# Expert weights laid eight rows to a partition in a two-layer diffusion step, with the down product from stationary weights

## The chip, the core and the metric

One core of a Trainium2 chip runs the whole step: TensorE (PE) with its weight loads (PEld), VectorE (DVE), ScalarE (ACT), GpSimd (POOL), SyncE (SP), and 16 DMA engines. The number of interest is the device time of one execution in microseconds; before the change the median of 3 runs is 2039.6 us. Everything is float32; PE runs each float32 product as two matmul instructions, each with its own weight load.

## The reference, cut to what matters

Two token sets, 128 context tokens and 512 latent tokens of width 1024, go through two layers. A layer is a combined input projection, a convolution module beside differential attention, an output projection, and a mixture of 16 experts in which each expert chooses 16 context rows and 64 latent rows. The convolution module and the experts are what the change touches:

```python
def conv_module(a, g, conv_w, conv_b, ln_g, ln_b):
    u = a * jax.nn.sigmoid(g)
    u = depthwise_conv(u, conv_w, width=31) + conv_b
    mu = jnp.mean(u, axis=-1); var = jnp.mean((u - mu) ** 2, axis=-1)      # over 512 channels
    return jax.nn.silu((u - mu) * lax.rsqrt(var + EPS) * ln_g + ln_b)

def expert_choice(h, w_router, w_gate, w_up, w_down):                      # per token set
    aff = jax.nn.softmax(h @ w_router)
    gsel, idx = lax.top_k(aff.T, C)                                        # C = 2*T/16 rows per expert
    xs = h[idx]                                                            # 80 rows over both sets
    hid = jax.nn.silu(xs @ w_gate[e]) * (xs @ w_up[e])                     # 1024 -> 1024
    ye = hid @ w_down[e] * gsel
    return zeros.at[idx].add(ye)                                           # every expert adds its rows
```

Each expert has three 1024x1024 matrices, 12.6 MB; both layers have 16 experts, 403 MB in all.

## The kernel before, in words

Tokens lie as 5 tiles of 128. The weights pass through `weight_ring`, six slots of 2 MB. SyncE issues all weight transfers, in the order of the code, each behind a wait that says that its slot is free.

**Projection.** `proj_unit` loads the input projection in five units of 512 columns. PE goes through 16 blocks (unit i, 128 columns b), in the order i then b: units 0 and 1 are the two halves of the gated convolution, units 2 and 3 keys and queries. For each block it does 512 latent and 128 context columns, and ACT copies the result out. From the ninth block on each block is followed by one unit of the modulation vectors (`block_modulation`). Five V blocks, one per token tile, follow (L500 before). DVE multiplies the gated halves (`glu_ready`), does the 31 taps over four chunks of 128 channels in place in `acc` (L1042), in between it rotates keys and queries (`rotate`). Behind the last V block come, one after the other: transposes of the context keys (L508), their copy by ACT (L815) into `key_rows`, which lies in `conv_tmp`, the store of it, and then, because the squares use `conv_tmp`, a wait for that store; PE's sums over channels for the mean (L519) and the squares (L527) with a matrix of ones; ACT's root, DVE's reciprocal (L1085) and product, ACT's SiLU (L834). Then attention begins, whose first exponential on ACT is the first L844.

**Experts.** An expert's weights are six units: gate and up for the first four row blocks, gate and up for the last four, and the two halves of down. `expert_src` lays row `k*128 + p` of a matrix on partition p, so a unit is 4 pieces of 4 KB on each partition. Unit i of the next expert is issued when unit i of this one is used (`expert_used`). The picked rows of the residual are gathered by POOL (80 rows of 4 KB), transposed on PE (L692), modulated by DVE. In gate and up (L706) the weights are stationary, 64 columns at a time on the two column halves of the array, and the 80 tokens move. In down (L722) the hidden rows are stationary (80 columns) and 512 weight columns move, so the result comes out with tokens on the partitions; DVE scales it (L1278) and POOL adds it to the residual in memory with an indirect DMA, then gathers for the expert after the next. PE's loop is `gate_up`, `picked_transposes(e + 1)`, `down`.

What sets the order is only the order of the code on each engine and the semaphores; there is no planner.

## Time and profile before

| what | value |
|---|---|
| median of 3 runs | 2039.6 us (2035.76 to 2039.83) |
| profiled execution, own time | 2046.08 us |
| its span, first to last instruction | 2044.3 us |
| PE busy / weight loads busy | 90% / 59% |
| DVE, ACT, POOL busy | 31%, 15%, 6% |
| bytes moved, mean rate | 534.68 MB, 262 GB/s |
| mean granted clock of PE | 0.951 |

The profile is of one execution. A busy PE is not a PE at its peak, since matmuls are pipelined and their ends are modelled. The page divides the span into 40 slices of 51 us; a digit is a busy share in tenths. The two long stretches of nines in the line of the DMA engines are the expert loops of the two layers.

### The profile page before, as it was taken

The numbers are of one execution on the slowest core, as the hardware profiler recorded it, in microseconds if no ns is written. First come the engines' busy times: TensorE is split into PE (matmuls) and PEld (weight loads), VectorE is DVE, ScalarE is ACT, GpSimd is POOL, SyncE is SP. The second block draws the span as 40 slices with busy tenths as digits, with TensorE's granted clock in tenths as the row PEclk, the third lists the DMA queues.
The fourth block names the chain that finished last, engine by engine and source line by source line (L and its number), as shares of the span: only waits on it lengthen the run. The fifth ranks groups of instructions, "written<-read, shape, count | busy, mean of one in ns | idle before, by whom it ended". The sixth has DMA issues, their size and how long they took to land.

```text
span 2044.3 us, 45797 instructions
## 1 busy us (share of the span) xinstructions
PE 1830.5 (90%) x21123; PEld 1202.4 (59%) x21123; DVE 632.7 (31%) x1044; ACT 306.6 (15%) x616; POOL 129.3 (6%) x157
## 2 busy tenths in 40 slices
PE   4999968894999999999949997789589999999993
PEld 2555436454676767767625553564376768677671
DVE  1159848234101101010120995752611011110101
ACT  2201145221000000000021112532200000000001
POOL 2000000000000000000010000000000000000001
PEclk9999989896999999999979999889799999999997
DMA  9336530233999999999931554004379999999995
GB/s 344 120 106 224 206 154 1 81 156 127 378 388 400 388 396 394 389 400 389 395 141 41 179 192 154 0 1 175 128 281 395 390 399 389 400 389 394 395 389 194
DMA packets 154438, 534.68 MB, mean 262 GB/s; under 512 B 5937, under 2 KB 6354, under 8 KB 154386
## 3 DMA queue, kind: packets, MB, share of 16 engines
q1 hardware_dynamic: 138880, 482.37, 61.3%
q0 software_dynamic: 12320, 42.47, 7.1%
q10 hardware_dynamic: 3186, 9.12, 1.1%
q8 instruction: 36, 0.59, 0.1%
q14 instruction: 16, 0.13, 0.0%
HBM read 509.30 MB, written 24.64 MB: 261 GB/s over the span
## 4 chain that ended last, share of the span: by engine, by line
PE 79%; DMA 8%; DVE 8%; ACT 1%; SPq 1%; issue 1%; POOL 0%; ACTq 0%; DVEq 0%; POOLq 0%
PE ps L706 25%; PE ps L722 19%; PE ps L488 14%; PE ps L618 7%; DMA weight_ring<-in_w_up_dram 5%; PE ps L500 3%; PE ps L432 2%; DVE neg_m L1112 2%; SPq L342 1%; PE ps L575 1%; PE ps L692 1%; PE ps L441 1%; PE ps L638 1%; DMA weight_ring<-in_conv_w_dram 1%; DMA out_dram<-conv_tmp 1%
## 5 line engine op out<-in xcount | busy, mean ns | idle before, releaser
L706 PEld LDWEIGHTS ps<-v_sb,weight_ring 128*64 128x64 f32 x16384 | 572.6, 138 | 37.5 <-issue 30.2
L706 PE MATMUL ps<-v_sb,weight_ring 128*64 128x80 f32 x16384 | 579.2, 234 | 11.6 <-DMA weight_ring<-in_w_up_dram 6.2
L722 PE MATMUL ps<-weight_ring,mix 128*80 128x512 f32 x1024 | 446.7, 594 | 0.0
L722 PEld LDWEIGHTS ps<-weight_ring,mix 128*80 128x80 f32 x1024 | 151.0, 150 | 272.5 <-issue 268.0
L488 PE MATMUL ps<-mix,weight_ring 128*128 128x128 f32 (+1 forms) x1024 | 284.5, 439 | 5.2 <-DVE mix L1012 5.2
L488 PEld LDWEIGHTS ps<-mix,weight_ring 128*128 128x128 f32 x1024 | 156.8, 192 | 142.0 <-issue 136.4
L1271 DVE TENSOR_TENSOR mix<-mix,ps 128x320 f32<-128x320 f32 x64 | 28.3, 483 | 544.3 <-PE ps L706 544.3
L1042 DVE SCALAR_TENSOR_TENSOR weight_ring<-u_gate,conv_cols,weight_ring 128x655 f32<-128x655 f32 x240 | 195.2, 898 | 0.0
L922 ACT ACTIVATE mix<-ps 128x320 f32<-128x320 f32 x64 | 24.5, 435 | 983.2 <-PE ps L706 983.2
L1278 DVE SCALAR_TENSOR_TENSOR qk<-ps,gsel,gate 80x1024 f32<-80x1024 f32 x32 | 41.0, 1280 | 392.3 <-PE ps L722 392.3
L618 PE MATMUL ps<-weight_ring,mix 128*128 128x512 f32 x320 | 144.6, 608 | 2.0 <-issue 2.0
L1401 POOL DMA_INDIRECT x_res<-qk,row_idx x32 | 45.9, 1434 | 979.9 <-DVE qk L1278 979.9
L618 PEld LDWEIGHTS ps<-weight_ring,mix 128*128 128x128 f32 x320 | 61.2, 195 | 74.3 <-issue 74.3
L500 PE MATMUL ps<-weight_ring,mix 128*128 128x512 f32 x160 | 70.5, 596 | 0.0
L1112 DVE TENSOR_REDUCE neg_m<-ps 128x2 f32<-128x1280 f32 (+1 forms) x40 | 50.8, 1274 | 17.4 <-PE ps L550 17.1
L844 ACT ACTIVATE weight_ring<-ps,neg_m 128x640 f32<-128x640 f32 (+1 forms) x80 | 55.7, 705 | 2.4 <-DVE neg_m L1112 2.3
L500 PEld LDWEIGHTS ps<-weight_ring,mix 128*128 128x128 f32 x160 | 29.8, 190 | 39.9 <-issue 39.9
L561 PE MATMUL ps<-ident,weight_ring 128*128 128x128 f32 x168 | 33.3, 305 | 22.0 <-DVE o_tok L1131 10.0
L432 PE MATMUL ps<-weight_ring,cond_silu 128*32 128x512 f32 x384 | 49.6, 637 | 0.8 <-issue 0.8
L1024 DVE TENSOR_TENSOR u_gate<-u_gate,conv_tmp 128x128 f32<-128x128 f32 (+1 forms) x16 | 7.2, 489 | 138.9 <-ACT conv_tmp L795 138.9
L575 PE MATMUL ps<-v_sb,weight_ring 128*128 128x128 f32 x272 | 45.4, 311 | 4.9 <-ACT weight_ring L862 4.8
L1171 DVE TENSOR_TENSOR conv_tmp<-ps,u_gate 128x1024 f32<-128x1024 f32 x10 | 12.2, 1224 | 103.7 <-PE ps L618 103.7
(176 smaller groups left out, 1185.8 us busy)
## 6 DMA issues: line engine op xcount, KB each, us to landing
weight_ring<-in_w_gate_dram SPq DMA_DIRECT2D x64, 2048.0 KB, 19.0
weight_ring<-in_w_up_dram SPq DMA_DIRECT2D x64, 2048.0 KB, 19.7
weight_ring<-in_w_down_dram SPq DMA_DIRECT2D x64, 2048.0 KB, 19.9
weight_ring<-in_w_mod_dram SPq DMA_DIRECT2D x24, 2048.0 KB, 8.2
weight_ring<-in_w_in_dram SPq DMA_DIRECT2D x10, 2048.0 KB, 12.8
weight_ring<-in_w_out_dram SPq DMA_DIRECT2D x4, 2048.0 KB, 10.6
x_res<-x_tile POOLq DMA_DIRECT2D x10, 512.0 KB, 3.3
x_unit<-x_norm ACTq DMA_DIRECT2D x10, 512.0 KB, 2.7
```

Source lines behind the costliest of these rows:

```text
L432: last = nc.tensor.matmul(ps[c * STRIP:(c + 1) * STRIP, 6, :], cond_silu[:, k, :], w[:, k, :], start=(k < 4), stop=(k >= 4))
L488: last = nc.tensor.matmul(ps[:, 2 * (n % 3) + bank, 0:cols.stop - cols.start], w[:, k, tokens(b)], mix[:, k, cols], start=(k == 0), stop=( ...
L500: last = nc.tensor.matmul(ps[:, 2 * (n % 3), :], mix[:, k, tokens(t)], w[:, k, :], start=(k == 0), stop=(k == KD - 1))
L575: last = nc.tensor.matmul(ps[:, 7, tokens(1)], a_col[:, tokens(j)], vals, start=(j == 0), stop=(j == n - 1))
L618: last = nc.tensor.matmul(ps[:, 2 * (i % 2) + n, :], mix[:, k, tokens(t)], w[:, k % 4, n * BANK:(n + 1) * BANK], start=(k == 0), stop=(k = ...
L706: last = nc.tensor.matmul(ps[c * HALF:(c + 1) * HALF, 2 * (i % 2) + f // BLK, f % BLK * CAP:(f % BLK + 1) * CAP], w[:, kk, o:o + HALF], pi ...
L722: last = nc.tensor.matmul(ps[0:CAP, 4 + n, :], hid[:, k, :], w[:, kk, n * BANK:(n + 1) * BANK], start=(k == 0), stop=(k == KD - 1))
L844: last = nc.scalar.activation(prob[:, b, m, 0:n], score_rows(s)[:, m, :], ACT.Exp, bias=neg_m[:, b, m:m + 1], accum_out=row_sum[:, b, m:m ...
L1042: ins = nc.vector.scalar_tensor_tensor(acc[:, j, :], src, w, acc[:, j, :], ALU.mult, ALU.add)
L1112: nc.vector.tensor_reduce(neg_m[:, s % 2, :], score_rows(s), AX, ALU.max, negate=True)\
L1278: nc.vector.scalar_tensor_tensor(added, ps[0:CAP, 4:6, :].rearrange("p b n -> p (b n)"), gsel[:, bass.ds(e, 1)], gate2[:], ALU.mult, ALU.m ...
L1401: nc.gpsimd.indirect_dma_start(out=x_res, out_offset=bass.IndirectOffsetOnAxis(ap=row_idx[:, e:e + 1], axis=0), in_=added, in_offset=None, ...
```

## The change

Six edits that belong together:

- A matrix of an expert is now laid with rows `8p` to `8p + 7` on partition p. Four of them are 16 KB in one piece, so a unit is one piece per partition. The contraction over rows then takes, for block k, the features `8q + k`; hidden features and picked rows follow: gate and up read their 64 stationary columns with a step of eight, and the picked rows, the normalized rows and the router's weights are read in the same order. The modulation vectors for it are brought into that order (`ROW_UNITS`, `par2_cols`).
- Down is computed as gate and up are: the weights stationary, 64 columns at a time, the 80 tokens moving. The result has features on the partitions; ACT copies its halves into `result_t`, PE transposes them back into the banks of the picked rows, and DVE takes them from there.
- PE's loop waits for the result of the expert before ahead of `picked_transposes`, because of those banks.
- The blocks of the projection go in the order of `BLOCK_LIST`: the gated pairs of the first two chunks come first. DVE does the taps of chunks 0 and 1, then those of 2 and 3.
- The sums for the mean stand behind V block 1, those of the squares behind V block 3; ACT and DVE follow. The cached keys are transposed before the V blocks.
- `key_rows` lies in the second half of `x_tile`, and POOL's load of that half waits for the store.

```diff
+BLOCK_LIST = ((0, 0), (1, 0), (0, 1), (1, 1), (0, 2), (0, 3), (1, 2), (1, 3)) + tuple(
+    (i, b) for i in (2, 3) for b in range(BLK))
-        key_rows = conv_tmp[:, 0, 0:BANK]
+        key_rows = x_tile[:, 1, 0:BANK]
             def expert_src(l, e, i):
                 w, half = (w_gate, w_up)[i % 2] if i < 4 else w_down, i // 2 if i < 4 else i - 4
-                return w[l, e].rearrange("(k p) n -> p k n", p=P)[:, half * 4:half * 4 + 4, :]
+                return w[l, e].rearrange("(p k) n -> p (k n)", p=P)[:, half * UNIT:(half + 1) * UNIT]
...
                 for i in range(2, 4):
-                    sp.wait_ge(*proj_done.at(l, BLK * (i - 1)))
+                    sp.wait_ge(*proj_done.at(l, block_no(i - 2, BLK - 1) + 1))
                     proj_unit(l, i)
...
-                for i in range(4):
-                    pe.wait_ge(*proj_loaded[i % 2].at(l, i // 2 + 1))
+                for n, (i, b) in enumerate(BLOCK_LIST):
+                    if b == 0:
+                        pe.wait_ge(*proj_loaded[i % 2].at(l, i // 2 + 1))
...
+                def conv_means():
+                    pe.wait_ge(*conv_ready.at(l, CH))
+                    if l == 0:
+                        pe.wait_ge(*past_copied.at(0, 1))
+                    for c0, c1, bank in ((LAT0, C_LEN, 1), (0, N_CTX, 3)):
+                        for j in range(CH):
+                            last = nc.tensor.matmul(ps[:, bank, 0:c1 - c0], ones[:], acc[:, j, c0:c1],
+                                                    start=(j == 0), stop=(j == CH - 1))
+                    last.then_inc(mean_ready.sem, 1)
+                def conv_squares():
+                    for j in range(CH):
+                        pe.wait_ge(*squared.at(l, j + 1))
+                        if j == 0:
+                            pe.wait_ge(*centred.at(l, CH))
+                        for c0, c1, bank in ((LAT0, C_LEN, 5), (0, N_CTX, 3)):
+                            last = nc.tensor.matmul(ps[:, bank, 0:c1 - c0], ones[:], conv_tmp[:, j % 2, c0:c1],
+                                                    start=(j == 0), stop=(j == CH - 1))
+                        last.then_inc(square_used.sem, 1)
...
                     block_modulation(l, n)
+                    if t == 1:
+                        conv_means()
+                    if t == 3:
+                        conv_squares()
...
-                                                   picked[:, tokens(k)], ident[0:CAP, 0:CAP])
+                                                   picked.rearrange("t (q k) -> t k q", k=KD)[:, k, :],
+                                                   ident[0:CAP, 0:CAP])
...
+                        cols = w.rearrange("p k (q f) -> p k f q", f=KD)
-                                        w[:, kk, o:o + HALF], picked_t[:, k, :],
+                                        cols[:, kk, f, c * HALF:(c + 1) * HALF], picked_t[:, k, :],
...
                 def down(e):
-                        for kk in range(KD // 2):
-                            k = half * (KD // 2) + kk
-                            for n in range(2):
-                                last = nc.tensor.matmul(ps[0:CAP, 4 + n, :], hid[:, k, :],
-                                                        w[:, kk, n * BANK:(n + 1) * BANK],
-                                                        start=(k == 0), stop=(k == KD - 1))
+                        for d in range(KD):
+                            for kk in range(KD // 2):
+                                k = half * (KD // 2) + kk
+                                for c in range(2):
+                                    o = d * P + c * HALF
+                                    last = nc.tensor.matmul(
+                                        ps[c * HALF:(c + 1) * HALF, 4 + d // BLK, d % BLK * CAP:(d % BLK + 1) * CAP],
+                                        w[:, kk, o:o + HALF], hid[:, k, :], ...)
+                            if half == 1 and d == BLK - 1:
+                                last.then_inc(result_lo_done.sem, 1)
                         last.then_inc(expert_used.sem, 1)
+                def result_transposes(e):
+                    pe.wait_ge(*picked_scaled.at(l, e + 2))
+                    for k in range(KD):
+                        if k % BLK == 0:
+                            pe.wait_ge(*result_copied.at(l, 2 * e + k // BLK + 1))
+                        last = nc.tensor.transpose(ps[0:CAP, 6 + k // BLK, tokens(k % BLK)], result_t[:, k, :], ident[:])
+                    last.then_inc(result_back.sem, 1)
                 with nc.Fori(0, EXPERTS, engines=[mybir.EngineType.PE], hint_back_edge=True) as e:
                     gate_up(e)
+                    pe.wait_ge(*result_taken.at(l, e + 1))
                     picked_transposes(e + 1)
                     down(e)
+                    result_transposes(e)
...
+                    for half in range(2):                                       # ACT, behind the SiLU
+                        ...
+                        nc.scalar.activation(result_t[:, half * BLK:(half + 1) * BLK, :], halves(4 + half), ACT.Copy)\
+                          .then_inc(result_copied.sem, 1)
...
-                act.wait_ge(*cache_stored.at(l, 2))
...
-                taps(0, TAPS // 2)
+                glu(0)
+                glu(1)
+                taps((0, 1), 0, TAPS)
+                glu(2)
+                glu(3)
+                taps((2, 3), 0, TAPS // 2)
                 rotate(0)
-                taps(TAPS // 2, TAPS)
+                taps((2, 3), TAPS // 2, TAPS)
...
-                    dve.wait_ge(*expert_used.at(l, e * 6 + 6))
+                    dve.wait_ge(*result_back.at(l, e + 1))
                     dve.wait_ge(*residual_written[0].at(l, e + 3))
-                    nc.vector.scalar_tensor_tensor(added, ps[0:CAP, 4:6, :].rearrange("p b n -> p (b n)"),
+                    nc.vector.scalar_tensor_tensor(added, ps[0:CAP, 6:8, :].rearrange("p b n -> p (b n)"),
...
-                for i in range(2):
-                    load_x(x_tile[:, i, :], l, OUT_TILES[i], x_loaded[i])
+                load_x(x_tile[:, 0, :], l, OUT_TILES[0], x_loaded[0])
+                pool.wait_ge(*cache_stored.at(l, 2))
+                load_x(x_tile[:, 1, :], l, OUT_TILES[1], x_loaded[1])
```

How rows move, at three places. A row is line, operation, result and operands, shape, count; the float32 doubling is not counted. First PE in layer 0 from the last V blocks on, before; L500 is a V block, L508 the key transposes, L417 the cached keys, L519 the mean, L527 the squares, L541 the first scores:

```order
L500 MATMUL ps<-weight_ring,mix 128x512 x8
L441 MATMUL ps<-pair_sum,x_tile 128x2 x4
L508 MATMUL ps<-ident,qk 128x128 x4
L417 MATMUL ps<-ident,x_norm 128x128 x8
L519 MATMUL ps<-weight_ring,ones 128x512 x4
L519 MATMUL ps<-weight_ring,ones 128x143 x4
L527 MATMUL ps<-conv_tmp,ones 128x512
L527 MATMUL ps<-conv_tmp,ones 128x143
L541 MATMUL ps<-qk 128x128 x6
```

and now, from V block 1 on (L547 a V block, L523 the mean, L534 the squares, L559 the key transposes, L575 the first scores):

```order
L547 MATMUL ps<-weight_ring,mix 128x512 x8
L464 MATMUL ps<-pair_sum,x_tile 128x2 x4
L445 MATMUL ps<-weight_ring,cond_silu 32x512 x8
L523 MATMUL ps<-weight_ring,ones 128x512 x4
L523 MATMUL ps<-weight_ring,ones 128x128 x4
L534 MATMUL ps<-conv_tmp,ones 128x512
L534 MATMUL ps<-conv_tmp,ones 128x128
L559 MATMUL ps<-ident,qk 128x128 x4
L575 MATMUL ps<-qk 128x128 x6
```

Between L523 and L534 stand two more V blocks with their modulation, and one behind L534. The mean and the squares have moved from behind the V blocks to between them, each with 15 columns fewer.

PE in the expert loop, before, from gate and up to the loop's end:

```order
L706 MATMUL ps<-v_sb,weight_ring 64x80 x256
L690 ISA
L692 MATMUL ps<-ident,qk 128x80 x8
L717 ISA
L722 MATMUL ps<-weight_ring,mix 80x512 x8
L717 REGISTER_ALU
L722 MATMUL ps<-weight_ring,mix 80x512 x8
L728 REGISTER_ALU
```

and now (L742 gate and up, L727 the picked rows, L759 down, L772 the transposes of the result):

```order
L742 MATMUL ps<-v_sb,weight_ring 64x80 x256
L725 ISA
L727 MATMUL ps<-ident,qk 128x80 x8
L752 ISA
L759 MATMUL ps<-mix,weight_ring 64x80 x64
L752 REGISTER_ALU
L759 MATMUL ps<-mix,weight_ring 64x80 x64
L772 MATMUL ps<-ident,mix 80x128 x8
L776 REGISTER_ALU
```

Down has 128 small products where it had 16 large ones, with the weights in the stationary place, and eight transposes behind them.

DVE in layer 0, before, from the last gated product to the second rotation (L1024 gating, L1037 and L1042 taps, L1053 to L1058 a rotation):

```order
L1024 TENSOR_TENSOR u_gate<-u_gate,conv_tmp 128x512
L1037 TENSOR_SCALAR weight_ring<-u_gate,conv_cols,par_cols 128x655 x4
L1042 SCALAR_TENSOR_TENSOR weight_ring<-u_gate,conv_cols,weight_ring 128x655 x56
L1053 STREAM_SHUFFLE weight_ring<-qk 128x512 x4
L1055 TENSOR_TENSOR qk<-qk,cos_sb 128x4x512
L1042 SCALAR_TENSOR_TENSOR weight_ring<-u_gate,conv_cols,weight_ring 128x655 x64
```

and now (L1100 gating, L1112 and L1117 taps, L1128 on a rotation):

```order
L1100 TENSOR_TENSOR u_gate<-u_gate,conv_tmp 128x512
L1112 TENSOR_SCALAR weight_ring<-u_gate,conv_cols,par_cols 128x655 x2
L1117 SCALAR_TENSOR_TENSOR weight_ring<-u_gate,conv_cols,weight_ring 128x655 x60
L1100 TENSOR_TENSOR u_gate<-u_gate,conv_tmp 128x128
L1112 TENSOR_SCALAR weight_ring<-u_gate,conv_cols,par_cols 128x655 x2
L1117 SCALAR_TENSOR_TENSOR weight_ring<-u_gate,conv_cols,weight_ring 128x655 x28
L1128 STREAM_SHUFFLE weight_ring<-qk 128x512 x4
L1117 SCALAR_TENSOR_TENSOR weight_ring<-u_gate,conv_cols,weight_ring 128x655 x32
```

The taps of two chunks now stand before the gating of the other two.

## Rows read from the trace of the kernel before

**Rows 1.** The page: busy tenths and GB/s in 40 slices of the span.
```profile
PE   4999968894999999999949997789589999999993
...
...
DMA  9336530233999999999931554004379999999995
GB/s 344 120 106 224 206 154 1 81 156 127 378 388 400 388 396 394 389 400 389 395 141 41 179 192 154 0 1 175 128 281 395 390 399 389 400 389 394 395 389 194
```

**Rows 2.** Chain of waits, layer 0, first two experts: start us, us, what.
```profile
495.82 20.09 PE ps L706 x512
...
530.55 17.86 PE ps L706 x512
...
549.11 13.94 PE ps L722 x32
```

**Rows 3.** The same chain, the last two experts of layer 0.
```profile
908.70 27.19 DMA weight_ring<-in_w_up_dram
...
976.53 26.51 DMA weight_ring<-in_w_up_dram
...
1022.39 0.03 issue
```

**Rows 4.** Busy time by window; last columns granted clock, DMA share, GB/s.
```profile
495.82:502.70 6.88, 6.88 (x140) 6.88 (x142) 0.00 (x0) 0.00 (x0) 0.00 (x0) 0.69 0.17 49
...
530.00:540.00 10.00, 10.00 (x276) 9.52 (x276) 1.28 (x1) 0.00 (x0) 2.41 (x2) 1.00 0.95 307
...
905.00:927.00 22.00, 22.00 (x254) 12.59 (x252) 3.72 (x5) 0.00 (x0) 2.34 (x2) 1.00 1.03 410
928.00:936.00 8.00, 7.13 (x208) 6.97 (x204) 0.00 (x0) 0.87 (x3) 0.00 (x0) 1.00 1.04 344
...
1018.00:1024.00 6.00, 4.38 (x11) 1.27 (x9) 1.28 (x1) 0.00 (x0) 0.00 (x0) 1.00 1.05 387
```

**Rows 5.** SyncE's own queue in the timeline: start us, us, what.
```profile
502.69 0.39 SPq L342 DMA_DIRECT2D weight_ring<-in_w_gate_dram  x1
...
908.70 4.16 SPq L342 DMA_DIRECT2D weight_ring<-in_w_up_dram  x1
```

**Rows 6.** Groups by form (layer 0's loop), and a row of the chain.
```profile
L922 ACT ACTIVATE mix<-ps 128x320 f32<-128x320 f32 x32 | 12.2, 435 | 491.5 <-PE ps L706 491.5
...
456.33 1.69 PE ps L638 x16
```

**Rows 7.** Chain of waits, layer 1, from the last V block to attention.
```profile
1249.79 3.45 PE ps L500 x8
...
1253.76 0.61 ACT conv_tmp L815
...
1254.39 7.48 DMA out_dram<-conv_tmp
...
1270.92 4.26 DVE weight_ring L1085
...
1276.08 4.47 ACT mix L834 x8
...
1280.57 1.28 ACT L844
...
1281.86 0.81 ACT weight_ring L844 x4
```

**Rows 8.** Chain (layer 0) and timeline (DVE's taps, layer 1's mean).
```profile
55.34 79.81 PE ps L488 x288
...
227.14 7.06 PE ps L500 x16
...
274.74 6.42 PE ps L527 x16
...
185.25 52.03 DVE L1042 SCALAR_TENSOR_TENSOR weight_ring<-u_gate,conv_cols,weight_ring 128x655 f32<-128x655 f32 x64
...
1253.91 4.68 PE L519 MATMUL ps<-weight_ring,ones 128*128 128x512 f32 x16 [0.25 <-ACT v_sb L806]
```

190 lines of the change are left out of this document (114 added, 76 removed).

## The prediction, made before the changed kernel was run

> **What bounds the kernel now.** I read the page's slices first, then the chain of waits in order of time, then the windows with the DMA rate. In the slices [rows 1] two long stretches, one per layer, have PE and DMA both at 9 and the rate at 378 to 401 GB/s: the expert loops, some 1,054 of 2,044 us (526.6 in layer 0, 495.82 to 1022.39, [rows 2, 3], and as much in layer 1). Which of the two engines bounds them the slices cannot say. The chain gives PE: an expert takes 17.86 (gate and up) + 0.70 (transposes of the picked rows) + 13.94 (down) = 32.50 us, over and over [rows 2]. But late in the loop it leaves PE: it waits for the last up unit, which landed at 908.70 + 27.19 = 935.89 and at 976.53 + 26.51 = 1003.04, two experts apart, so the weights come at 33.58 us an expert [rows 3]. That is the true period. Weights alone move at 410 GB/s, 2 MB in 5.12 us, and while the scatter and gather of rows are in flight at 344 [rows 4]; 6 x 5.12 = 30.7, so the row transfers cost 2.9 us an expert. The DMA falls 1.08 us behind PE per expert, and the one expert of weights held in the ring hides that until the end. SyncE shows it too: an issue takes 0.39 us at 502.69 and 4.16 us at 908.70, as if its queue were full [rows 5]. So **the expert loops are DMA-bound**, and a faster PE alone gains there only at the two ends.
>
> Outside, the chain has a stretch in which PE is nearly idle: from the end of the last V block (1249.79 + 3.45 = 1253.24) to the first exponential (1281.86) 28.6 us pass in layer 1 [rows 7], and the same steps stand in layer 0: a copy of the keys, 7.48 us of waiting for its store, squares, root, reciprocal, normalization, SiLU, one after the other.
>
> **The change, part by part.** All sums are made on the profiled execution: span 2044.3, own time 2046.08, which is 6.5 over the median of 2039.6; I carry the difference over to the median.
>
> *Convolution norm inside the V blocks.* PE now does the sums for the mean (4.68 us, [rows 8]) after V block 1 and those of the squares (6.42, [rows 8]) after block 3. The last V block thus ends 4.7 + 6.4 = 11.1 us later, in layer 1 at 1264.3. The squares end one block earlier, at 1264.3 - 7.9 = 1256.4. Table load 1.28 and root 0.9 on ACT: 1258.6; reciprocal 4.26 on DVE: 1262.9; first normalized quarter 0.85 later, 1263.7, so it is ready before ACT is free of the last V copy, 1264.9. Then table load 1.28, SiLU 4.47, key copy 0.61 and table load 1.28: first exponential at 1272.5 instead of 1281.86, 9.3 us earlier. Layer 0 has the transposes of the cached keys and some constants in the same line, which moves a little of it; I take 8.5 there. The store of the keys is no longer waited for, since they lie in x_tile. Its cover: the load of the second x_tile half now waits for that store, about 100 us before its use. The sum needs DVE to be done with the taps by V block 1. They ended at 185.25 + 52.03 = 237.3, 64 of them at 0.81 us each [rows 8]. With the new block order two gated chunks are ready after four blocks instead of eight, at 55.34 + 4 x 8.87 + 1.2 = 92 (nine blocks took 79.81); 62 taps end near 142, the other half with the first rotation between near 205, the second rotation near 224, and PE gets to the mean at 227.14 + 7.06 + 3.7 = 238 [rows 8]. If that cover failed, each us would be paid in full on PE. Together **-17.8 us**.
>
> *Down from stationary weights.* It leaves 32 instructions of 436 ns (13.94 us) and adds 256 of the form of gate and up, 128x64 stationary and 80 columns moving; 512 of these take 17.86, so 8.93 us. Added behind it: ACT's copy of the last 320 columns (435 ns, [rows 6]), four transposes of about 0.11 us (16 matmul instructions with 128 stationary columns took 1.69 us, [rows 6]), two semaphore hops: 1.4 us. PE period 17.86 + 0.70 + 8.93 + 1.4 = 28.9. DVE's gated result waits for the transposes, and the scatter for it; both have some 20 us to spare inside the loop. What it gains is at the ends. At the start: from the first reload's issue at 502.69 [rows 5] to 1003.04 the DMA brought 14.67 experts' units, 34.1 us each instead of 33.58, so 7.8 us were lost in the first expert or two. Some of it is the first transfer's own delay; some is that units 4 and 5 came free late (530 to 540: share 0.95 and 307 GB/s, where rows and weights together give 344, [rows 4]). With down 5 us shorter I take 2.5 us a layer. At the end the last unit lands two units after 1003.04, at 1013.3, and PE ended at 1022.39; now 1013.3 + 4.5 + 1.4 = 1019.2: 3.2 a layer. **-11.4 us** for both layers.
>
> *16 KB pieces.* A unit was 512 pieces of 4 KB, now 128 of 16 KB. No row shows 16 KB, but rows of two sizes bound it [rows 4]: 2 KB pieces (the input projection) go at 387 GB/s (84.7 ns a piece on each of 16 engines), 4 KB at 410 (159.8 ns). The difference, 75.1 ns for 2 KB, leaves 10 ns fixed per piece. 16 KB: 10 + 8 x 75.1 = 611 ns, 429 GB/s, a unit in 4.89 us. If a 16 KB piece is handled as four of 4 KB nothing is gained (5.12); if long pieces read in steps of 32 KB suit the memory less, the nearest row is the 2 KB rate, 5.42. I take 4.92, a little short of this line through two points. 0.20 us x 90 units (15 reloads of 6) x 2 layers: **-36 us**. The period becomes 6 x 4.92 + 2.9 = 32.4, over PE's 28.9, so it stays DMA-bound with 3.5 us to spare.
>
> *Gate and up columns with a step of eight.* Each of 512 weight loads an expert now takes every eighth column, 32 bytes apart. No row of this trace has such a read. Today two halves of 64 columns and their matmuls pass in 2 x 34.9 = 69.8 ns. A load of 128 packed columns is seen at 1.69/16 = 106 ns, so 64 take 53 and are hidden under 67 ns of 80 moving columns. From below, the strided load costs nothing (nor can it gain, the matmul being the longer). From above, it takes twice the time: 106 ns for a pair of halves, if they still load side by side. It would begin to count at 83 ns a pair, where PE reaches 32.4. I take zero. The strided transposes of picked and normalized rows (8 an expert, 8 a token tile) go the same way at a tenth of the size.
> The Trainium skill speaks against this part: "Advanced Engine Details and Errata", section Memory Cachelines, says that SBUF has lines of 16 bytes, that at least two hits on one are needed to absorb the access latency, and that going to another line with each access costs. Four-byte elements 32 bytes apart hit each line once. By that rule the upper bound holds; what it makes of the time is the second rival below. No row here shows it either way.
>
> *Small edits* (layout of the second modulation and norm vectors, four more short loads at 35 us, the wait for the third projection unit two blocks later): the unit is issued two blocks, 17.7 us, before its use, more than three times the 5.4 us that its bytes take. Nothing.
>
> **Sum**: 17.8 + 11.4 + 36 = 65; 2046.1 - 65 = 1981 for a profiled execution, **1974** for the median.
>
> **Rivals.**
> *A. The pieces gain nothing* (chance 0.22). The queue cuts them to 4 KB, or the rate is capped elsewhere. For: the rows have two sizes only, and both lie between 387 and 410. Against: the fixed part between them. Time: 2039.6 - 29 = 2010.
> The Trainium skill, "DMA: Bandwidth & Descriptors", section SWDGE vs HWDGE vs iDMA, puts a packet at 4096 bytes by preference; by that rule this rival wins. The trace neither agrees nor disagrees: it has no piece above 4 KB.
> *B. The strided weight load is paid* (0.16), the slower side. For: nothing hides more than 17 ns of a pair's load. Against: nothing in the trace. Price: 256 pairs x (106 + 3) ns = 27.9 us instead of 17.86, PE period 38.9. A layer's loop runs 16 x 38.9 + 2.2 (the slow first expert, 20.09 against 17.86 [rows 2]) = 625 instead of 526.6 from first matmul to last. 2 x 98 - 18 = +178: 2218. It decides from 83 ns a pair on; just past it the change is worth about the first and last terms only.
> *C. The row transfers interleave better or the fixed part is larger* (0.07): a unit at 4.8, time near 1950.
> *D. Longer pieces are read more slowly* (0.05): at 5.42 a unit, 0.3 x 180 = 54 - 29 = +25: 2065.
> *E. PE's waits gather in one gap.* While rows are in flight a unit needs 7.8 us and PE 4.5, so it idles 3.3 us once an expert. The granted clock was 0.69 in the first 6.9 us of the loop, behind a stretch in which PE had waited, and 1.00 after it [rows 4]: 1.2 and 2.4 GHz in turn. If each expert pays the 2.2 us of the first, PE needs 31.1, under 32.4; only the ends lose 2 or 3 us. Inside the range.
>
> **Chances and range.** Forecast with its spread (unit 4.85 to 5.05) 0.50, A 0.22, C 0.07, B 0.16, D 0.05. About 0.2% (4 us) is what a measurement of this kernel can tell from no change. Slower: B and D, 0.20, with 0.02 given back because a load only partly slowed is hidden: 0.18. Same: 0.03. Faster: 0.79. The range 1950 to 2034 holds the forecast, A and most of C; B stays outside.
>
> **What would show it.** Right: DMA issues of 16 KB pieces landing 4.9 us apart late in a loop, near 425 GB/s; the chain in the loop going through weight transfers and SyncE, no longer through PE; PE rows of 128x64 with a mean as before and pairs 70 ns apart; PE idle some 3 us an expert, waiting for the last up unit; first exponential 8.5 to 9.3 us earlier after the projection's start. Wrong: packets of 4 KB in the size line (A); gate and up over 21 us an expert with the chain in PE throughout (B); V blocks waiting for DVE's taps.

## The result, and the profile after

| what | before | after |
|---|---|---|
| median | 2039.0 us (4 runs) | 2335.6 us (4 runs, 2334.5 to 2341.45) |
| ratio of the runs | | 1.146, 95% interval 1.144 to 1.149 |
| profiled execution, own time | 2046.08 us | 2334.59 us |
| its span | 2044.3 us | 2332.6 us |
| PE busy / weight loads busy | 90% / 59% | 92% / 77% |

The change made the kernel 14.6% slower; 1974 was forecast, with a range to 2034. Rival B named the mechanism and undersized it (2218). Where a kernel's executions fell into a faster and a slower group, as only those of experiment ten did, its time and ratio below are those of the faster group.

The page's slices, which answer to [rows 1]:

```profile
PE   4999888879999999999959997895999999999994
...
DMA  9156403348888888888622613043788888888872
GB/s 355 53 190 231 171 13 126 135 173 318 306 316 307 300 327 308 303 324 303 241 87 86 214 70 127 1 167 131 296 317 314 300 327 307 300 322 301 314 291 96
```

In the loops PE still stands at 9, but the DMA engines have fallen to 8 and to 300 to 327 GB/s. The loops are no longer bound by the weights. The chain of waits in layer 0's loop (start us, us, what; answers to [rows 2, 3]) says by what:

```profile
526.91 31.28 PE ps L742 x511
558.19 1.04 PE ps L727 x8
559.23 9.00 PE ps L759 x256
568.24 1.17 PE ps L772 x8
569.41 0.04 issue
569.45 31.27 PE ps L742 x511
```

It never leaves PE. Gate and up (L742) take 31.27 us where they took 17.86 [rows 2], that is 122.1 ns for each of 256 pairs of halves instead of 69.8. Down (L759) takes 9.00, against 13.94 before and 8.93 as worked out. An expert needs 42.54 us (526.91 to 569.45) where the weights had set 33.58.

The groups by form name the instruction (line, engine, operation, tiles, shape, count | busy us, mean ns | idle before):

```profile
L742 PEld LDWEIGHTS ps<-v_sb,weight_ring 128*64 128x64 f32 x16384 | 996.8, 218 | 13.3 <-issue 13.3
L742 PE MATMUL ps<-v_sb,weight_ring 128*64 128x80 f32 x16384 | 1001.5, 285 | 5.2 <-DVE v_sb L1350 3.9
L759 PEld LDWEIGHTS ps<-mix,weight_ring 128*64 128x64 f32 x8192 | 285.5, 137 | 3.3 <-issue 0.7
L759 PE MATMUL ps<-mix,weight_ring 128*64 128x80 f32 x8192 | 290.9, 233 | 0.5 <-issue 0.5
```

The same load, 128 rows by 64 columns of float32, has a mean of 137 ns from packed columns (down) and of 218 from every eighth column (gate and up). Loads and matmuls overlap, so a mean is not the time between two starts. But the load's busy time, 996.8 us, has become as long as the matmul's, which is what to expect if the load now paces the pair; experiment one tests it. The copy of the result on ACT costs 438 ns in the mean, where 435 was taken from its neighbour [rows 6].

A window in the loop (PE, PEld, DVE, ACT, POOL busy; then granted clock, DMA share, GB/s; answers to [rows 4]):

```profile
530.00:540.00 10.00, 10.00 (x170) 10.00 (x170) 0.00 (x0) 0.00 (x0) 1.61 (x2) 1.00 1.01 315
```

The clock is granted in full (1.00) there, as it was before; it is not the cause. PEld was busy 9.52 of 10 us in the window at 530 before, now 10.00. SyncE's queue and the issues answer to [rows 5]:

```profile
925.58 0.33 SPq L355 DMA_DIRECT2D weight_ring<-in_w_up_dram  x1
```

```profile
weight_ring<-in_w_gate_dram SPq DMA_DIRECT2D x64, 2048.0 KB, 7.5
```

Late in the loop an issue takes 0.33 us where it took 4.16, and over the whole run a gate unit lands 7.5 us after its issue (median) where it took 19.0: little is queued ahead of it.

The convolution's end in layer 1, in the chain, answers to [rows 7, 8]:

```profile
1397.28 4.49 PE ps L534 x16
1401.77 6.88 PE ps L547 x16
...
1408.67 0.60 ACT v_sb L874
...
1417.23 0.82 ACT weight_ring L905 x4
```

The wait for the store and the reciprocal have gone out of the chain. From the end of the last V block to the first exponential 8.6 us pass (1408.65 to 1417.23) where 28.6 did.

**The account.** The stretches between five marks (the projection's first matmul, first and last exponential, first matmul of the loop and last of down), in both profiled executions:

| stretch, us | before L0, L1 | after L0, L1 | difference |
|---|---|---|---|
| start to projection | 55.3 | 50.3 | -5.0 |
| projection to first exponential | 236.4, 224.9 | 229.9, 218.7 | -12.7 |
| exponentials, and on to the loop | 204.1, 206.5 | 203.6, 204.7 | -2.3 |
| expert loop | 526.6, 527.0 | 679.9, 680.7 | +307.0 |
| behind the loop | 33.3, 30.2 | 33.6, 31.3 | +1.4 |

The mark "first exponential" is here the start of its table load, 1.3 us ahead of the exponential itself. The sum is +288.4, the difference of the spans 288.3. The first row is no effect: over the kernels below this stretch lasts 50.2 to 56.7 us without a pattern. The second scatters as well, by some 1.7 us a layer between kernels that have the same code there. All that was lost was lost in the loop.

### The profile page after: what moved, and what is told of

Its sections match the earlier page's. It is cut to its first block, busy times and chain, and to the rows that moved or that the text cites. A ratio compares the mean times of both kernels' runs of the same rounds, so it can differ in the third digit from the quotient of the medians.

```text
span 2332.6 us, 60929 instructions
## 1 busy us (share of the span) xinstructions
PE 2141.9 (92%) x28611; PEld 1795.3 (77%) x28611; DVE 636.0 (27%) x1063; ACT 335.3 (14%) x690; POOL 131.3 (6%) x161
## 4 chain that ended last, share of the span: by engine, by line
PE 88%; DVE 7%; DMA 2%; ACT 1%; issue 1%; POOL 0%; ACTq 0%; DVEq 0%; POOLq 0%
PE ps L742 43%; PE ps L759 12%; PE ps L510 12%; PE ps L652 6%; PE ps L547 3%; PE ps L445 2%; PE ps L772 2%; PE ps L727 2%; DVE neg_m L1197 1%; PE ps L609 1%; PE ps L673 1%; DMA weight_ring<-in_conv_w_dram 1%; PE ps L458 1%; DVE weight_ring L1233 1%; PE ps L595 1%
## 5 line engine op out<-in xcount | busy, mean ns | idle before, releaser
L742 PEld LDWEIGHTS ps<-v_sb,weight_ring 128*64 128x64 f32 x16384 | 996.8, 218 | 13.3 <-issue 13.3
L742 PE MATMUL ps<-v_sb,weight_ring 128*64 128x80 f32 x16384 | 1001.5, 285 | 5.2 <-DVE v_sb L1350 3.9
L759 PE MATMUL ps<-mix,weight_ring 128*64 128x80 f32 x8192 | 290.9, 233 | 0.5 <-issue 0.5
L759 PEld LDWEIGHTS ps<-mix,weight_ring 128*64 128x64 f32 x8192 | 285.5, 137 | 3.3 <-issue 0.7
L1117 DVE SCALAR_TENSOR_TENSOR weight_ring<-u_gate,conv_cols,weight_ring 128x655 f32<-128x655 f32 x240 | 195.3, 894 | 0.0
L983 ACT ACTIVATE mix<-ps 128x320 f32<-128x320 f32 x64 | 24.5, 434 | 769.8 <-PE ps L742 769.8
L991 ACT ACTIVATE mix<-ps 128x320 f32<-128x320 f32 x64 | 28.0, 438 | 532.3 <-PE ps L759 532.3
L547 PE MATMUL ps<-weight_ring,mix 128*128 128x512 f32 x160 | 70.6, 595 | 0.0
L547 PEld LDWEIGHTS ps<-weight_ring,mix 128*128 128x128 f32 x160 | 29.7, 190 | 36.5 <-issue 36.5
L595 PE MATMUL ps<-ident,weight_ring 128*128 128x128 f32 x168 | 32.8, 300 | 22.3 <-DVE o_tok L1216 10.0
L727 PE MATMUL ps<-ident,qk 80*128 80x80 f32 x272 | 38.2, 286 | 9.7 <-DMA qk<-x_unit,row_idx 9.7
```

Source lines behind the costliest of these rows:

```text
L547: last = nc.tensor.matmul(ps[:, 2 * (n % 3), :], mix[:, k, tokens(t)], w[:, k, :], start=(k == 0), stop=(k == KD - 1))
L595: last = nc.tensor.transpose(dst, a_row[:, s % 2, tokens(j)], ident[:])
L727: last = nc.tensor.transpose(ps[:, 6 + k // 4, (k % 4) * CAP:(k % 4 + 1) * CAP], picked.rearrange("t (q k) -> t k q", k=KD)[:, k, :], iden ...
L742: last = nc.tensor.matmul(ps[c * HALF:(c + 1) * HALF, 2 * (i % 2) + f // BLK, f % BLK * CAP:(f % BLK + 1) * CAP], cols[:, kk, f, c * HALF: ...
L759: last = nc.tensor.matmul(ps[c * HALF:(c + 1) * HALF, 4 + d // BLK, d % BLK * CAP:(d % BLK + 1) * CAP], w[:, kk, o:o + HALF], hid[:, k, :] ...
L1117: ins = nc.vector.scalar_tensor_tensor(acc[:, j, :], src, w, acc[:, j, :], ALU.mult, ALU.add)
```

## The experiments

Medians stand against 2038 to 2040 us for the kernel before, measured beside them. Experiments two to six are one execution each. The cuts of code show the lines that matter; `...` stands for other lines, and where nothing else is said they are against the changed kernel.

### One: the columns packed, all else as changed

```diff
-                                        cols[:, kk, f, c * HALF:(c + 1) * HALF], picked_t[:, k, :],
+                                        w[:, kk, f * P + c * HALF:f * P + (c + 1) * HALF], picked_t[:, k, :],
```

> The changed kernel with one edit: gate and up read 64 adjacent columns (o = f*128 + c*64) instead of every eighth; all pieces stay 16 KB, down, transposes and order stay. The hidden features then meet other rows of the down matrix, so the output is not the reference's; the work is the same in number and shape. Theory 1 (the strided weight load is what costs, 122 ns a pair of halves instead of 70): the L742 row goes back to 234 ns per matmul, gate and up to 17.9 us, PE's period to 17.9 + 1.05 + 9.0 + 1.2 = 29.1, the loop is again bounded by the weights, at 32.4 us an expert if a 16 KB piece takes 611 ns, and the time is 2335.6 - 2 x 16 x (42.54 - 32.4) = 2011 at the most and, with the ends of the loop, near 1985. Rival 2 (long pieces written into the ring disturb PE's reads, whatever their step): gate and up stay near 31 us and the time near 2335. Rival 3 (down, its transposes and their waits cost more than worked out): the time stops well above 2011.

Measured 2008.8 us, ratio 0.985 (0.983 to 0.987). The group and a stretch of the chain:

```profile
L741 PEld LDWEIGHTS ps<-v_sb,weight_ring 128*64 128x64 f32 x16384 | 590.6, 140 | 74.1 <-DMA weight_ring<-in_w_up_dram 51.4 <-issue 17.6 <-DMA weight_ring<-in_w_gate_dram 2.9
```

```profile
546.14 18.14 PE ps L741 x512
...
878.94 4.67 PE ps L741 x128
...
883.63 29.42 DMA weight_ring<-in_w_up_dram
913.05 0.04 issue
913.09 4.67 PE ps L741 x128
```

The load is back to 140 ns and gate and up to 18.1; the loop waits for weights again. One index expression is worth 327 us. Rivals 2 and 3 fall. But 2008.8 lies at the upper end of what was expected: the other terms of the forecast are also smaller than they were made. In the profiled execution the two loops gained 27.8 us, where pieces and down together were to give 47.4; the stretch from the projection to the first exponential gained 11.1 instead of 17.8; and 5.9 us were lost behind the loops. The later runs look for those.

### Two to four: which step

The pattern of the changed kernel with a step of two, four and sixteen:

```diff
-                        cols = w.rearrange("p k (q f) -> p k f q", f=KD)
+                        cols = w.rearrange("p k (g q s) -> p k g s q", q=HALF, s=2)   # and s=4, s=16
...
-                                        cols[:, kk, f, c * HALF:(c + 1) * HALF], picked_t[:, k, :],
+                                        cols[:, kk, (2 * f + c) // 2, (2 * f + c) % 2, :], picked_t[:, k, :],
```

> The changed kernel with gate and up reading every second column (8 bytes apart) instead of every eighth; the hidden features come in another order, so the output is not the reference's. If what counts is how many of the 64 columns lie on one 16-byte line (theory 1a, two per line here), this is as packed: 70 ns a pair, time near 1985. If the cost grows evenly with the distance (1b), a pair takes 70 + 52 x 4/28 = 77 ns, gate and up 19.8 us, still under the weights, and the time is the same; the two part by the L742 mean and the chain. If any step but one is paid in full (1c): 122 ns a pair, 2335.

> The same with every fourth column (16 bytes apart); output again not the reference's. 1a (lines of 16 bytes, one column per line): as slow as the step of eight, 122 ns a pair, near 2335. 1b (even growth with distance): 70 + 52 x 12/28 = 92 ns a pair, gate and up 23.6 us, PE period 34.9, about 2335 - 32 x 7.6 = 2092. 1c: 2335.

> The same with every sixteenth column (64 bytes apart, 64 columns span the whole row of 1024); output not the reference's. 1a: every column is on a line of its own at a step of eight as well, so no more is paid: near 2335. 1b: 70 + 52 x 60/28 = 181 ns a pair, gate and up 46 us, PE period 57.6, about 2335 + 32 x 15 = 2815. If the cost is that of lines of 32 or 64 bytes, this is slower than a step of eight and the step of four faster.

Measured 2007.1, 2323.7 and 2258.2 us. An expert's gate and up in the chains of the three kernels, in this order:

```profile
555.04 18.00 PE ps L742 x512
```

```profile
568.71 30.95 PE ps L742 x512
```

```profile
559.96 28.84 PE ps L742 x512
```

| step, bytes | 4 | 8 | 16 | 32 | 64 |
|---|---|---|---|---|---|
| ns per pair of halves | 70.9 | 70.3 | 120.9 | 122.1 | 112.7 |

It is a threshold between 8 and 16 bytes, not a growth with distance: 1b and 1c fall. Nor is a step of two merely hidden behind the matmul: its loads have a mean of 142 ns, where packed ones have 140. The Trainium skill's rule in "Advanced Engine Details and Errata", section Memory Cachelines (lines of 16 bytes, at least two hits on one), gives just this threshold, and the trace agrees for float32. Why 64 bytes are a little cheaper than 32 stays open; 1a had 2335 there, and 2258 was measured.

### Five: do the two halves load side by side

```diff
-                                        cols[:, kk, f, c * HALF:(c + 1) * HALF], picked_t[:, k, :],
+                                        (cols[:, kk, f, 0:HALF] if c == 0 else w[:, kk, f * P + HALF:(f + 1) * P]), picked_t[:, k, :],
```

> The changed kernel, but of each pair of column halves only the first is read with a step of eight, the second from 64 adjacent columns; the output is not the reference's. If the two halves load side by side (as the prediction took it), the pair lasts as long as its slower load: 122 ns, gate and up 31.3 us, time near 2335. If loads go one after the other, 61 ns for a strided one and at most 35 for a packed one: 96 ns a pair or less, gate and up 24.6 us, PE period 35.9, about 2335 - 32 x 6.7 = 2121.

Measured 2338.8 us, the same as with both strided. The chain and the group:

```profile
574.26 31.34 PE ps L742 x384
```

```profile
L742 PEld LDWEIGHTS ps<-v_sb,weight_ring 128*64 128x64 f32 x16384 | 999.1, 177 | 12.9 <-issue 12.9
```

The mean of the loads falls to 177 ns, the mean of 137 and 217, but the pair does not shorten (31.34 / 256 = 122.4 ns): it lasts as long as the slower half. They load side by side, and on a half that reads with a stride a load follows the one before it after 122 ns. Experiment twelve shows nearly the same figure, 120 ns, where strided loads stand one after the other and only two columns move.

### Six: the stride alone, in the kernel before

```diff
+                        cols = w.rearrange("p k (q f) -> p k f q", f=KD)
...
-                                        w[:, kk, o:o + HALF], picked_t[:, k, :],
+                                        cols[:, kk, f, c * HALF:(c + 1) * HALF], picked_t[:, k, :],
```

> The kernel before with one edit: gate and up read every eighth column; pieces of 4 KB, down, order as before. Output not the reference's (the hidden features meet other rows of down). Theory (the stride alone, wherever the weights lie and however they came): gate and up 31.3 us, PE's period 31.3 + 0.7 + 13.9 = 45.9, loop 737 us instead of 526.6, the whole 2039.6 + 421 = 2460. Rival (long pieces written at the same time are part of it): gate and up below 30 us, time under 2420.

Measured 2449.2 us. The chain and a window of 300 us in the loop:

```profile
536.29 31.21 PE ps L706 x512
567.50 0.70 PE ps L692 x8
568.20 13.93 PE ps L722 x32
```

```profile
600.00:900.00 300.00, 300.00 (x3566) 236.44 (x3564) 24.80 (x34) 14.34 (x21) 14.04 (x12) 1.00 0.81 288
```

31.21 us with 4 KB pieces is as good as 31.27 with 16 KB: the price belongs to the read alone. The period is 45.84, and 2449 stands against 2460 worked out.

### Seven and eight: the order alone, and with the stationary down

The first has the experts wholly as before and only the projection's order and the convolution sums as changed; the second adds the stationary down, still with 4 KB pieces and no strided read. The edits that both share; left out are the packed reads in gate and up and in the transposes and, in the first, down as it was before:

```diff
-ROW_UNITS = (6, 7, 8, 9)
+ROW_UNITS = ()
...
-                return w[l, e].rearrange("(p k) n -> p (k n)", p=P)[:, half * UNIT:(half + 1) * UNIT]
+                return w[l, e].rearrange("(k p) n -> p k n", p=P)[:, half * 4:half * 4 + 4, :]
...
```

> The reference's own computation: the expert part wholly as before (4 KB pieces, packed columns, hidden rows stationary in down); only the order of the projection, the sums of the convolution norm between the V blocks and the key rows in x_tile are the new ones. Predicted for this part: -17.8. Measured in the changed kernel from the projection's start to the first exponential: -6.5 in layer 0 and -6.2 in layer 1, with four strided modulation units a layer in it, each 1.06 us longer. Without those: -10.7 a layer and 2039.6 - 21 = 2018 (rival: the strided modulation is not the difference, and it stays at -12.7: 2027).

> The reference's own computation with 4 KB pieces for all three matrices, no strided read anywhere (columns, transposes, modulation), down from stationary weights and the new projection order. Theory: the loop is bound by the weights at the old 33.58 us an expert; against before only down at the ends (predicted 5.7 a layer) and the order (measured 6 a layer, and some us at the start) are left: 2039.6 - 11 - 12 - 5 = 2011 if the prediction's ends hold. Rival (the gain in the loop of the kernel with packed columns, 16.1 and 11.7 us by layer, came from 16 KB pieces): some 2020 or more. Rival (it came from down): the same 2009 as that kernel.

Measured 2016.0 (ratio 0.988, 0.985 to 0.992) and 2015.5 (0.988, 0.986 to 0.991), where 2018 and 2011 were expected. The order alone takes 23.7 us off, and down adds nothing that can be told. From the projection to the first exponential the order has 225.0 and 213.7 us: -11.4 and -11.2 against before, where 8.5 and 9.3 were forecast. In the changed kernel this stretch gained only 12.7 us over both layers; the strided modulation gave back most of the difference, as experiment twelve confirms (groups by form of the changed kernel, 64 strided columns and 128 packed ones):

```profile
L458 PEld LDWEIGHTS ps<-pair_sum,x_tile 128*64 128x64 f32 x128 | 16.0, 216 | 2.2 <-issue 1.5
L464 PEld LDWEIGHTS ps<-pair_sum,x_tile 128*128 128x128 f32 x128 | 15.9, 192 | 9.2 <-ACT x_tile L804 7.3 <-issue 1.9
```

Here only two columns move, so nothing hides the load, and half the columns with a stride take longer than all of them packed.

Where down's gain went the chains behind layer 0's loop show. With the order alone:

```profile
997.05 13.96 PE ps L760 x32
...
1013.29 7.41 DMA x_res<-qk,row_idx
...
1023.17 9.10 DMA qk<-x_res
```

and with the stationary down:

```profile
994.93 4.65 PE ps L761 x128
999.58 1.18 PE ps L774 x8
...
1003.05 7.89 DMA x_res<-qk,row_idx
...
1013.41 11.85 DMA qk<-x_res
```

The loop is 6.0 and 4.5 us shorter. But behind it stand the transposes (1.18), and the last scatter and the reload of the residual take 7.89 + 11.85 instead of 7.41 + 9.10; they now start earlier. There they meet the next layer's weights, still in flight. What the queues moved during the reload, first with the order alone, then with the stationary down (q0 is POOL's, the reload itself; q1 is SyncE's, the weights):

```profile
q0 software_dynamic: 720, 2.62, 72.3%
q1 hardware_dynamic: 157, 0.29, 8.7%
```

```profile
q0 software_dynamic: 720, 2.62, 55.8%
q1 hardware_dynamic: 646, 1.29, 28.8%
```

The reload is the same 2.62 MB; 1.00 MB more of weights pass beside it, which at some 400 GB/s is 2.5 us of its 2.75 us more. Behind the loop it takes 38.7 us instead of 34.1 in layer 0, and 31.4 instead of 29.8 in layer 1. Of the 10.5 us that the loops gained, 4.3 are left behind them; the medians show 0.5, and an effect of this size is within their scatter.

### Nine: 16 KB pieces for gate and up, down in 4 KB, packed

```diff
+                if i >= 4:
+                    return w[l, e].rearrange("(k p) n -> p k n", p=P)[:, half * 4:half * 4 + 4, :]
                 return w[l, e].rearrange("(p k) n -> p (k n)", p=P)[:, half * UNIT:(half + 1) * UNIT]
...
-                                        cols[:, kk, f, c * HALF:(c + 1) * HALF], picked_t[:, k, :],
+                                        w[:, kk, f * P + c * HALF:f * P + (c + 1) * HALF], picked_t[:, k, :],
```

> The reference's own computation, with packed columns: gate and up are laid eight rows to a partition (16 KB pieces) and read 64 adjacent columns; the hidden features are then in their plain order, so down goes back to rows k*128 + p, four 4 KB pieces. Down from stationary weights, the order of the projection and the strided transposes and modulation stay. With the theory (the strided weight load is the whole loss) PE's period is 29.1 us as in the kernel with packed columns and 16 KB pieces throughout (2008.8), and a third of the units goes back to 4 KB: if a unit of 4 KB pieces costs 0.2 us more, 30 x 2 x 0.2 = +12 us, 2021. If piece size is worth nothing (the gain of that kernel all came from PE and the order): 2009. If the strided load was not all and the pairing of rows in down hid something: over 2040.

Measured 2015.4 us (ratio 0.988, 0.985 to 0.990): between the cases, and the same as 4 KB throughout. But that comparison mixes two things. This kernel still has the strided modulation, and from the projection to the first exponential it takes 229.9 and 220.3 us, 11.5 in all over experiment eight, where its loops are 2.5 and 6.4 us shorter (516.9 and 516.0 against 519.5 and 522.4). The pieces gain in the loop what the modulation loses outside.

### Ten and eleven: 8 KB pieces in down

With a step of two, a pair of neighbouring hidden features lies on one partition, and down can be loaded two rows at a time. First as two transfers of 64 partitions, against the kernel of experiment nine:

```diff
-                    return w[l, e].rearrange("(k p) n -> p k n", p=P)[:, half * 4:half * 4 + 4, :]
+                    return w[l, e].rearrange("(g c q s) n -> c q g (s n)", c=2, q=HALF, s=2)[:, :, half * 2:half * 2 + 2, :]
...
+                    for c in range(2):
+                        sp.dma_start(dst[c * HALF:(c + 1) * HALF, :].rearrange("p (g n) -> p g n", g=2),
+                                     expert_src(l, e, i)[c]).then_inc(expert_loaded[i].sem, 16)
...
-                                        w[:, kk, f * P + c * HALF:f * P + (c + 1) * HALF], picked_t[:, k, :],
+                                        pairs[:, kk, 2 * (f // 2) + c, f % 2, :], picked_t[:, k, :],
```

> The reference's own computation again: since a step of two was as fast as packed, gate and up read every second column of a group of 128; then two neighbouring hidden features lie on one partition in two blocks, and a row pair of down is one 8 KB piece (two per partition and unit, as two transfers of 1 MB). Gate and up stay in 16 KB pieces. Theory (piece size counts by a fixed part of 10 ns): 8 KB takes 310 ns, most of the way from 160 x 4 to 611 per 16 KB; the time is 2009 + 4 = 2013, some 8 under the kernel with 4 KB pieces in down. If piece size counts for nothing: equal to it. If the two more SyncE issues per expert matter: slower than it.

Measured 2351 us, ratio 1.159 (1.153 to 1.165), a loss whose size no theory had. Then as one transfer:

```diff
-                    for c in range(2):
-                        sp.dma_start(dst[c * HALF:(c + 1) * HALF, :]..., expert_src(l, e, i)[c])...
+                    dst = dst.rearrange("p (g n) -> p g n", g=2)
+                sp.dma_start(dst, expert_src(l, e, i)).then_inc(expert_loaded[i].sem, 16)
```

> The kernel with 8 KB pieces in down once more, but a unit of down is one transfer of 2 MB over all 128 partitions instead of two of 1 MB over 64 each. In the version with two, the loop took 742 and 740 us and a transfer of 1 MB landed 4.7 to 5 us behind the one before it, as long as one of 2 MB over 128 partitions elsewhere. Theory (a transfer into only half of the partitions moves at half the rate): now 8 KB pieces do between 4 and 16 KB, the weights come at about 32.9 us an expert (33.1 with 4 KB in down, 32.8 with 16 KB throughout, by the landings), and the time is 2015.4 - 7 = 2008. Rival (8 KB pieces, or a source address that jumps between two groups of 64 rows, are slow in themselves): again far above 2040.

Measured 2005.1 us (0.983, 0.981 to 0.986), 10.3 below the kernel with 4 KB in down, where 7 were expected; the two loops are 10.1 us shorter. The window of 300 us in layer 0's loop, in this order: 4 KB throughout; 16 and 4 KB; 16 and 8 KB as two transfers; the same as one; 16 KB throughout:

```profile
600.00:900.00 300.00, 274.34 (x7059) 263.83 (x7057) 33.53 (x45) 26.44 (x46) 21.08 (x18) 0.97 1.03 394
```

```profile
600.00:900.00 300.00, 280.88 (x7199) 270.67 (x7196) 36.88 (x49) 26.31 (x45) 21.07 (x18) 0.97 1.02 400
```

```profile
600.00:900.00 300.00, 208.59 (x4645) 200.82 (x4642) 22.89 (x30) 17.54 (x30) 14.04 (x12) 0.86 0.98 284
```

```profile
600.00:900.00 300.00, 279.44 (x7276) 270.25 (x7272) 36.87 (x49) 26.31 (x45) 21.08 (x18) 0.98 1.01 403
```

```profile
600.00:900.00 300.00, 280.87 (x7287) 270.29 (x7284) 35.62 (x46) 28.46 (x48) 22.52 (x20) 0.98 1.01 404
```

An expert moves 12.58 MB of weights and 0.33 MB of rows out and in again, 13.24 MB; by the last column its period is 33.6, 33.1, 46.6, 32.9 and 32.8 us. So by the rate 16 KB pieces are worth 0.8 us an expert, not 1.2. In time they gave less: the two loops are 16.1 us (experiment one) to 19.1 us (experiment eleven) shorter than with 4 KB throughout (experiment eight). The pieces themselves took what had been worked out. In the same 300 us the median record of a 16 KB piece is 615 ns, where 611 was taken, and of an 8 KB piece 314, where 310 was.

The two half transfers leave the DMA share at 0.98 and move 284 GB/s. SyncE's queue in that window, with two transfers and then with one (packets, MB, share of the 16 engines):

```profile
q1 hardware_dynamic: 7546, 80.79, 91.1%
```

```profile
q1 hardware_dynamic: 10290, 115.15, 93.3%
```

Nearly the same busy share moved 81 MB instead of 115. The median record of an 8 KB piece is 618 ns instead of 314, so a half transfer of 1 MB takes as long as a whole one of 2 MB. The two additional issues of SyncE an expert, a rival of this run, are not the cause: the engines are not idle but slow. The Trainium skill, "SBUF — State Buffer", section Door 1: The DMA port swizzle, says that a transfer into partitions 0 to 63 reaches half of the ports and in the limit gets half of the rate; the trace agrees. It is most of the loss: 4.86 us more for each of the two units, over 30 reloads, are an estimate of 292 of the 346 us between the two medians. The rest stays open; in the profiled run, which is the longest (2464 us, the others down to 2344, granted clock 0.86 in the window), the 16 KB pieces beside them had become slower too, 717 ns in the mean where 625 with one transfer.

### Twelve: the modulation put in order by ACT

Against the kernel of experiment eleven:

```diff
-                    rows = mod_rows.rearrange("r (q k) -> r k q", k=KD)
+                    rows = mod_rows.rearrange("r (k q) -> r k q", k=KD)
...
-                nc.scalar.activation(mod_rows, ps[:, 6, :], ACT.Copy).then_inc(mod_rows_copied.sem, 1)
+                src, dst = ps[:, 6, :], mod_rows
+                if MOD_LIST[l][u][1] in ROW_UNITS:
+                    src = src.rearrange("r (q k) -> r k q", k=KD)
+                    dst = dst.rearrange("r (k q) -> r k q", k=KD)
+                nc.scalar.activation(dst, src, ACT.Copy).then_inc(mod_rows_copied.sem, 1)
```

> The same, and the modulation rows of the four units that PE reads with a step of eight are brought into the new order by ACT when it copies them out of PSUM (a read with a step of 32 bytes, written packed); PE then reads 64 adjacent columns. Theory (the strided load on PE cost 5 to 6 us a layer between the projection's start and the first exponential: 229.9 and 220.3 against 225.0 and 213.7 with the plain order): 8 to 11 us under its sister, near 2000. Rival (ACT pays for the stride what PE saves: its copy of 0.60 us would have to become 1.6): no difference.

Measured **1997.5 us**, ratio 0.980 (0.978 to 0.983), 7.6 below the kernel of experiment eleven, just under the 8 to 11 expected, and the lowest of all. The groups:

```profile
L463 PEld LDWEIGHTS ps<-pair_sum,x_tile 128*64 128x64 f32 x128 | 8.1, 138 | 2.2 <-issue 1.5
...
L813 ACT ACTIVATE x_tile<-ps 128x512 f32<-128x512 f32 x24 | 14.3, 597 | 55.8 <-PE ps L450 55.8
```

PE's load falls from 216 to 138 ns, and ACT's 24 copies keep their mean of 597 ns, eight of them strided among them. From the projection to the first exponential: 226.1 and 214.7 us instead of 231.5 and 220.3. The intervals of the two ratios overlap (0.981 to 0.986 and 0.978 to 0.983); the 5.4 and 5.6 us of this stretch are the surer sign.

One unit's loads in the timeline, strided (the changed kernel) and packed (this one):

```profile
212.16 2.00 PEld L458 LDWEIGHTS ps<-pair_sum,x_tile 128*64 128x64 f32 x16
```

```profile
210.28 1.01 PEld L463 LDWEIGHTS ps<-pair_sum,x_tile 128*64 128x64 f32 x16
```

Both at a granted clock of 1.00, with nothing to wait for: the starts of the strided loads are 120 ns apart, of the packed ones 58.

## Why the prediction was wrong

- **Failed step: "Gate and up columns with a step of eight ... I take zero."** It costs 13.4 us an expert on PE (31.27 us instead of 17.86), takes the loop's bound from the weights to PE, and makes each loop 165 to 169 us longer than packed columns (680 against 510.5 and 515.3). Its reasoning named the right place (17 ns of cover over a packed load of 53 ns) and then had no row for the load itself. Of two bounds it took the lower, and gave the upper 0.16, though the one rule that bore on it spoke for the upper. With a gain of 65 us at stake and a bound 244 us above the forecast, that was the number to doubt.
- **The upper bound was none, and not for its factor.** "Twice the time, 106 ns" came from a row of packed loads of 128 columns, halved and doubled. Measured alone, a packed load of 64 follows the last after 58 ns, not 53, and a strided one after 120, twice as long (experiment twelve); in gate and up a pair takes 122. With 31.3 for 27.9 us, and 1.04 for 0.70 in the strided transposes, the period is 42.5 instead of rival B's 38.9, and 2218 becomes some 2334, next to the 2335.6 measured. So close a hit has some luck in it: the projection gained 5.1 us less than this sum takes, and the stretch ahead of it was 5.0 us shorter by chance.
- **Rival A falls.** The page counts 24631 packets of 8 KB or more, where there were 52 before, and the 16 KB pieces moved as such. The preferred packet of 4096 bytes that the prediction cites for this rival does not hold for these transfers: SyncE issues them, and where it and the trace differ the trace decides.
- **The term of the pieces: right in sign, two thirds of its size as a rate and half in time.** The period was to fall from 33.58 to 32.4 us and fell to 32.8 where packed columns let it; of 36 us in the two loops 16 to 19 came. The unit itself was right (8 pieces of 615 ns on each engine are 4.92 us, as taken). What is left of the period, 32.8 - 6 x 4.92 = 3.3 us, is the step that was off: the rows were to go on costing 2.9. In the changed kernel the term is worth nothing, since PE bounds.
- **The term of down: right on PE (9.00 for 8.93, 1.17 + 0.04 for 1.4), and given back at the ends.** Its 5.7 us a layer came as 6.0 and 4.5 in the loop; 4.6 and 1.6 of them return behind it, which the prediction had no line for.
- **The convolution: right, and larger than forecast** when alone (-22.6 for -17.8), -12.7 in the changed kernel. The fall from V block to exponential was -20.0 in layer 1 for -20.4. What failed beside it is that the layout of the second modulation was put at nothing among the small edits: its strided loads cost 1 us a unit on PE's path (2.01 against 1.01), and there are 8 units. The strided transposes of the picked rows cost 0.34 us an expert. The squares took 4.49 us instead of 6.42.
- **Rival E** was rightly put inside the range: in the packed loops PE waits, and the granted clock is 0.97 or 0.98 over 300 us. What it costs was not measured by itself.
- **The signs to look for** named the case well: over 21 us an expert in gate and up, with the chain in PE throughout, was what stood there.

## What to carry to other kernels

Before a layout that trades long DMA pieces for a strided read, ask which engine reads it, and how many of its elements lie within 16 bytes: on TensorE's weight load of float32 a step of 8 bytes was free, and with 16 bytes the pair took 1.7 times as long. A step of two let the pieces of down grow from 4 to 8 KB without any cost on PE, and a copy that another engine makes anyway can carry the reordering (here ACT's, at no cost). If the decisive operation has no row in the trace, do not give its lower bound more than even chances because it is the nearer number.

## What was not expected of the hardware

- The strided weight load has a threshold and then hardly depends on the distance: 70.3 ns a pair at 8 bytes, 120.9 at 16, 122.1 at 32, 112.7 at 64 (one execution each but the third).
- A transfer into 64 partitions took as long as one of twice the bytes into 128 (618 instead of 314 ns for a piece of 8 KB), while the share of busy DMA engines stayed at 0.98: a high share is not a high rate.
- ACT read PSUM with a step of 32 bytes at the speed of a packed read (597 ns for 512 columns either way).
